# Three pairs of chunks by seven block products in the last stage, their later weight sums by accumulating DMAs

## The chip, the cores and the metric

The kernel runs on one core of a Trainium2 chip. The metric is the device time of one execution in microseconds, of the slowest core (there is one). Five engines with their own in-order queues work side by side: TensorE (PE) multiplies, VectorE (DVE), ScalarE (ACT) and GpSimd (POOL) do elementwise work, SyncE (SP) issues most DMAs. They wait for each other by semaphores only.

## The reference, cut to what matters

Two transformer blocks in float32 on x of 1 x 256 x 1024. The last stage, which the change is about, is the squared-ReLU MLP that ends the second block:

```python
h2 = rmsnorm_2(x, norm_mlp_g[l])                                             # 256 x 1024
up = jnp.square(jax.nn.relu(jnp.einsum('bsd,df->bsf', h2, w_up[l])))         # w_up 1024 x 4096
x = x + jnp.einsum('bsf,fd->bsd', up, w_down[l])                             # w_down 4096 x 1024
```

The two gated stages, which the change touches at their ends only, are `h + 0.5 * swiglu(rmsnorm(h), w_gu, w_down)` with 2816 hidden columns.

## The kernel before

**Split products.** Every float32 weight tile of 128 x 4 x 512 (1 MB, a *unit*) is used as hi + lo: ScalarE copies it to a rounded type (`split_hi`, L1101 to L1114), VectorE subtracts (`split_lo`, L1816 to L1822). A product of a block is then three matmuls for each of four 128-row slices (`portion`, L2628 to L2658): hi x hi, lo weight, lo data. So a unit used for one token half is 12 matmuls of 512 columns, for both halves 24. hi and lo lie in a ring of three slots for all units in order: `split_hi(n)` waits until TensorE is through with unit n - 3 (`used`, n - 2).

**The last stage.** The 4096 hidden columns are eight chunks of 512. A chunk costs two *up* units (two halves of the 1024 input rows) and two *down* units. A chunk's result is squared by ScalarE, written as 16-bit planes (`planes_from`, L1346), turned by a DMA transpose on SyncE (`flip_last`, L721), merged by VectorE (`last_merge`, L2093) and split again (`last_hi`, L1378, `last_lo`, L2103) before its down units. `last_order` (L106) fixes TensorE's order by hand; down units of two chunks earlier stand between the up work.

**Pairs.** `PAIRS` names the chunks i for which i and i + 1 are computed together: the 2 x 2 blocks of tokens and columns, with the input rows in two halves, by seven products of blocks instead of eight (`product`, L2854). Products p1, p2 and p3 take a loaded block of w_up; p5, p6, p7 and p4 take sums of blocks, T1 to T4, made by VectorE in place in six buffers `last_operand` (`weight_sum`, L1869 to L1889: buffer 4 = 2 + 0, 5 = 3 + 4, 2 = 3 + 2, 1 = 1 + 5). Partial results pass through PSUM bank G[0] and `xn`: ScalarE's `keep` (L1178) copies the bank after p1, p6 and p7; p6, p7 and p4 then add on to the same bank, and TensorE waits for the copy before each; VectorE's `add_product` (L1916) adds p2, p5 and p3; `square` (L1365) squares the four finished blocks. Before, chunks 2 and 3 and chunks 6 and 7 are such pairs; 0, 1, 4 and 5 are plain. In this text u(i,b) and d(i,b) are up and down units.

**What sets the order.** `pair_chunks` and `plain_chunks` write out ScalarE's order (L1388, L1424) and VectorE's (L2118, L2153) by hand; SyncE's order of loads and transposes is a list (L950 to L993). In a pair that is not the first, ScalarE has before: d(i-2,0), keep 0, p6, d(i-2,1), square 0, p7, last_hi(i-1), keep 1, p5, p4, keep 2; VectorE: d(i-2,0), add 0, p6, d(i-2,1), merge(i-1), p7, T4, last_lo(i-1), p5, p4. GpSimd has no work in this stage. The first three sums of the second pair are made in the plain chunks before it.

**The gated stages' ends.** SyncE loads the last down units, then the first unit of w_in for the next stage, and then issues the two transposes of chunk 9 (L864 to L869, L922 to L927), whose merge is L1939, whose lo is L1947 and whose matmuls are L2806.

Of the kernel before, what the change touches and what calls it, by code (L numbers as in the profile page):

```python
# [42 lines left out]
W = 512  # L43
# [34 lines left out]
PAIRS = (2, 6)  # L78
# [49 lines left out]
LAST_PAIR = len(PAIR_AT) - len(PAIRS)  # L128

# [176 lines left out]
class Pairs:  # L306


    def __init__(self, sem):
        self.b_in = [sem(f"pairs_b_in{j}") for j in range(4)]  # L310
        self.t_made = sem("pairs_t_made")
        self.s_made = sem("pairs_s_made")
        self.s_hi = sem("pairs_s_hi")
        self.s_lo = sem("pairs_s_lo")
        self.kept = sem("pairs_kept")
        self.added = sem("pairs_added")


def program(nc, a, out):
    ctx = ExitStack()  # L320
    with ctx:
# [327 lines left out]
        def _(sp_eng):  # L649
# [34 lines left out]
            def block_free(j, b):  # L684
# [3 lines left out]
                elif PAIR_AT[j][1] == PAIRS[1] or j in (1, 3):  # L688
# [49 lines left out]
            def gated_weights(w_gu, w_down, f, beside=lambda k: None):  # L738
# [62 lines left out]
                dn(10)  # L801

# [61 lines left out]
            for c, (first, width, _) in enumerate(IN1):  # L864
                for half in range(2):
                    columns(a["w_in"], U_M1 + 2 * c + half, first, half, width)
                    if (c, half) == (0, 0):
                        flip(ffns[0], 9, 1)
                        flip(ffns[0], 9, 0)  # L869
# [50 lines left out]
            for c, (first, _) in enumerate(IN2):  # L920
                for half in range(2):
# [3 lines left out]
                    if (c, half) == (0, 0):  # L925
                        flip(ffns[1], 9, 1)
                        flip(ffns[1], 9, 0)  # L927
# [33 lines left out]
            last_block(LAST_PAIR + 1, 0)  # L961
            last_load("d", 1, 1)
            last_load("u", 4, 0)
            flip_last(2, 0)
            last_block(LAST_PAIR + 1, 2)
            last_block(LAST_PAIR + 1, 1)
            last_load("u", 4, 1)
            flip_last(2, 1)
            last_block(LAST_PAIR + 1, 3)
            last_load("d", 2, 0)  # L970
            flip_last(3, 1)
            flip_last(3, 0)
            last_load("d", 2, 1)
            last_load("u", 5, 0)
            last_load("u", 5, 1)
            flip_last(4, 0)
            flip_last(4, 1)
            last_load("d", 3, 0)
            last_load("d", 3, 1)
            last_load("d", 4, 0)  # L980
            flip_last(5, 0)
            last_load("d", 4, 1)
            flip_last(5, 1)
            last_load("d", 5, 0)
            last_load("d", 5, 1)
            last_load("d", 6, 0)
            flip_last(6, 0)
            last_load("d", 6, 1)
            flip_last(6, 1)
            last_load("d", 7, 0)  # L990
            flip_last(7, 1)
            flip_last(7, 0)
            last_load("d", 7, 1)  # L993
# [93 lines left out]


        @block.scalar
        def _(act):  # L1090
# [10 lines left out]
            def split_hi(n, width=W):  # L1101
# [5 lines left out]
                elif KINDS[n] in OPERAND:  # L1107
                    act.wait_ge(pairs.t_made, 4 * pair_of(n) + {"p5": 1, "p6": 2, "p7": 3, "p4": 4}[KINDS[n]])
# [279 lines left out]
            def pair_chunks(j):  # L1388

                i = PAIR_AT[j][1]  # L1390
                split_hi(unit_of("d", i - 2, 0))
                if j == LAST_PAIR:
                    plain_planes(1, 0)
# [26 lines left out]
                last_hi(i)  # L1420
                square(j, 3)
                split_hi(unit_of("d", i - 1, 1) + 2)

            def plain_chunks(i):  # L1424

                split_hi(unit_of("d", i - 2, 0))
                last_hi(i - 1)
                split_hi(unit_of("d", i - 2, 1))
                plain_planes(i, 0)
                split_hi(unit_of("u", i + 1, 0))  # L1430
                plain_planes(i, 1)
                split_hi(unit_of("u", i + 1, 1))
                split_hi(unit_of("d", i - 1, 0))
                last_hi(i)
                split_hi(unit_of("d", i - 1, 1))
                plain_planes(i + 1, 0)
                split_hi(unit_of("d", i - 1, 1) + 1)
                plain_planes(i + 1, 1)
                split_hi(unit_of("d", i - 1, 1) + 2)

            def last_ffn():
# [9 lines left out]
                for i in range(2, NF2, 2):  # L1451
                    if i in PAIRS:
                        pair_chunks(PAIR_AT.index((2, i)))
                    else:
                        plain_chunks(i)
# [351 lines left out]
        def _(dve):  # L1807
# [61 lines left out]
            def weight_sum(j, t):  # L1869
# [10 lines left out]
                elif t == 2:  # L1880
                    dve.wait_ge(pairs.b_in[3], UNIT_IN * (j + 1))
                elif t == 4:
                    dve.wait_ge(pairs.b_in[1], UNIT_IN * (j + 1))
                    dve.wait_ge(lo_done, pair_unit(j, "p2") + 1)
                if t > 1:
                    dve.wait_ge(pairs.t_made, 4 * j + t - 1)
# [231 lines left out]
            def pair_chunks(j):  # L2118

                i = PAIR_AT[j][1]  # L2120
                split_lo(unit_of("d", i - 2, 0))
                if j == LAST_PAIR:
                    for m in (3, 2, 4):
                        sum_lo(2, m)
# [3 lines left out]
                    weight_sum(j, 4)  # L2128
                    split_lo(unit_of("p7", i))
                    last_merge(i - 1)  # L2130
                else:
# [5 lines left out]
                    weight_sum(j, 4)  # L2137
                    last_lo(i - 1)
                split_lo(unit_of("p5", i))
                if j == LAST_PAIR:  # L2140
# [9 lines left out]
                last_lo(i)  # L2150
                split_lo(unit_of("d", i - 1, 1) + 2)

            def plain_chunks(i):  # L2153

                j = LAST_PAIR + len([x for x in PAIRS if x < i])
                split_lo(unit_of("d", i - 2, 0))
                last_merge(i - 1)
                weight_sum(j, 1)
                split_lo(unit_of("d", i - 2, 1))
                last_lo(i - 1)  # L2160
                split_lo(unit_of("u", i + 1, 0))
                weight_sum(j, 2)
                split_lo(unit_of("u", i + 1, 1))
                last_merge(i)
                split_lo(unit_of("d", i - 1, 0))
                weight_sum(j, 3)
                last_lo(i)
                split_lo(unit_of("d", i - 1, 1))
                split_lo(unit_of("d", i - 1, 1) + 1)
                split_lo(unit_of("d", i - 1, 1) + 2)  # L2170

            def last_ffn():
# [8 lines left out]
                for i in range(2, NF2, 2):  # L2181
                    if i in PAIRS:
                        pair_chunks(PAIR_AT.index((2, i)))
                    else:
                        plain_chunks(i)
# [438 lines left out]
        def _(pe):  # L2624
# [208 lines left out]
            def plain_up(i):  # L2833

                for u in range(2):
                    n = unit_of("u", i, u)
                    use(n)
                    for t in range(NT):
                        if i > 1 and u == 0 and i % 2 == 0:

                            if t == 0:
                                pe.wait_ge(last.acted, acted_before(i))
                            else:
                                pe.wait_ge(pairs.added, 3 * (LAST_PAIR + len([x for x in PAIRS if x < i])) - 2)
                        elif i > 1 and u == 0 and t == 0:

# [417 lines left out]
```

## Time and profile before

| | us |
|---|---|
| median of 3 runs | 980.93 (980.13 to 981.02) |
| the profiled execution, its own time | 980.98 |
| its span in the trace | 979.2 |
| TensorE busy | 971.3 |
| VectorE busy | 764.8 |
| ScalarE busy | 658.5 |
| GpSimd busy | 117.4 |

Times in the trace count from the span's start. A timeline row gives the start, the duration, the engine, the line and the operation with its tiles, and in brackets how long the engine was idle before it and what released it. Matmuls overlap in the pipeline, so a row's duration (0.39 us) is longer than the distance between two starts. Instructions on ScalarE and VectorE overlap too by about 0.1 us.

### The profile page before, as it was taken

How to read it: one execution, taken by the hardware profiler on the slowest of the kernel's cores; microseconds unless marked ns; L12 is line 12 of the kernel's file. 1: busy time of each engine (PE TensorE's matmuls, PEld its weight loads, DVE VectorE, ACT ScalarE, POOL GpSimd, SP SyncE). 2: the span in 40 equal slices, each digit the busy share in tenths (PEclk: the TensorE clock that was granted, in tenths of full speed). 3: DMA queues.
4: the chain of work that ended last, by engine and by line, in shares of the span. 5: the costliest groups of instructions: out<-in, count | busy, mean ns of one | idle time of the engine just before them, and what ended most of it. 6: DMA issues, size and time to landing. Idle time of an engine off the chain costs nothing.

```text
span 979.2 us, 12257 instructions
## 1 busy us (share of the span) xinstructions
PE 971.3 (99%) x4528; PEld 796.9 (81%) x4528; DVE 764.8 (78%) x1010; ACT 658.5 (67%) x887; POOL 117.4 (12%) x109
## 2 busy tenths in 40 slices
PE   8999999999999999999999999999999999999998
PEld 7788888888777788888888788888888888888887
DVE  5898797768987666888797677787689878977675
ACT  7766575677666536766566586868875548877782
POOL 0000000022300000000000041169903001000000
PEclk9999999999999999999999999999999999999999
DMA  8998948696444546986926587667666654695532
GB/s 262 314 294 281 281 122 240 199 320 196 133 151 148 172 129 215 260 268 213 267 67 213 180 243 230 164 181 208 201 214 215 239 191 151 210 321 172 189 111 94
DMA packets 167589, 202.12 MB, mean 206 GB/s; under 512 B 58081, under 2 KB 113770, under 8 KB 167402
## 3 DMA queue, kind: packets, MB, share of 16 engines
q1 hardware_dynamic: 166938, 201.21, 65.9%
q8 instruction: 36, 0.59, 0.2%
q14 instruction: 23, 0.19, 0.1%
q10 hardware_dynamic: 592, 0.14, 0.1%
HBM read 182.45 MB, written 5.77 MB: 192 GB/s over the span
## 4 chain that ended last, share of the span: by engine, by line
PE 91%; DVE 2%; DMA 2%; issue 1%; ACT 1%; SPq 1%; POOL 0%; ACTq 0%; DVEq 0%
PE bank L2653 22%; PE bank L2655 22%; PE bank L2654 22%; PE bank L2806 4%; PE bank L2808 4%; PE bank L2807 4%; PE bank L2924 3%; PE bank L2925 3%; PE bank L2926 3%; DMA halves_t<-halves 2%; PE bank L2668 1%; PE bank L2960 1%; PE bank L3075 1%; DMA raw<-in_ffn_w_gu 1%; DVE lo L1838 0%
## 5 line engine op out<-in xcount | busy, mean ns | idle before, releaser
L2653 PE MATMUL bank<-hi,xh 128*128 128x512 f32 (+1 forms) x824 | 328.2, 398 | 1.0 <-DVE lo L2254 0.9
L2655 PE MATMUL bank<-hi,xl 128*128 128x512 f32 (+1 forms) x824 | 320.7, 389 | 0.0
L2654 PE MATMUL bank<-lo,xh 128*128 128x512 f32 (+1 forms) x824 | 320.1, 388 | 0.0
L1821 DVE TENSOR_TENSOR lo<-raw,hi 128x2048 fp32r<-128x2048 f32 (+1 forms) x87 | 198.5, 2287 | 60.8 <-ACT hi L1114 60.5
L1114 ACT ACTIVATE hi<-raw 128x2048 fp32r<-128x2048 f32 (+1 forms) x90 | 170.6, 1902 | 83.7 <-PE bank L2655 36.7
L2653 PEld LDWEIGHTS bank<-hi,xh 128*128 128x128 f32 x824 | 154.9, 188 | 34.4 <-issue 2.7
L2655 PEld LDWEIGHTS bank<-hi,xl 128*128 128x128 f32 x824 | 154.8, 188 | 32.7
L2654 PEld LDWEIGHTS bank<-lo,xh 128*128 128x128 f32 x824 | 155.1, 188 | 29.7
L1838 DVE TENSOR_TENSOR lo<-raw,hi 128x1024 fp32r<-128x1024 f32 (+1 forms) x108 | 132.2, 1234 | 43.4 <-ACT hi L1123 42.9
L1123 ACT ACTIVATE hi<-raw 128x1024 fp32r<-128x1024 f32 x102 | 104.5, 1051 | 10.1 <-PE bank L2655 10.1
L2806 PE MATMUL bank<-hi,hh 128*128 128x512 f32 x176 | 69.2, 393 | 1.2 <-DVE hl L1947 1.2
L2808 PE MATMUL bank<-hi,hl 128*128 128x512 f32 x176 | 68.6, 390 | 0.0
L2807 PE MATMUL bank<-lo,hh 128*128 128x512 f32 x176 | 68.5, 389 | 0.0
L1821 DVE TENSOR_TENSOR lo<-first_operand,hi 128x2048 fp32r<-128x2048 f32 x28 | 64.1, 2288 | 3.6 <-ACT hi L1114 3.5
L1114 ACT ACTIVATE hi<-first_operand 128x2048 fp32r<-128x2048 f32 x28 | 53.6, 1916 | 17.0 <-PE bank L2655 11.8
L1025 POOL TENSOR_TENSOR small<-small 128x1 f32<-128x1 f32 x10 | 8.5, 851 | 366.4 <-DVE small L1845 346.4
L2925 PE MATMUL bank<-lo,last_hh 128*128 128x512 f32 (+1 forms) x130 | 50.1, 386 | 0.0
L2926 PE MATMUL bank<-hi,last_hl 128*128 128x512 f32 (+1 forms) x130 | 50.1, 386 | 0.0
L2924 PE MATMUL bank<-hi,last_hh 128*128 128x512 f32 (+1 forms) x130 | 50.1, 386 | 0.0
L1032 POOL TENSOR_TENSOR rstd_q<-ss_q,small 128x8 f32<-128x8 f32 x16 | 34.6, 2166 | 88.5 <-DVE ss_q L2331 88.3
L2806 PEld LDWEIGHTS bank<-hi,hh 128*128 128x128 f32 x176 | 33.1, 188 | 8.5 <-issue 2.0
L1821 DVE TENSOR_TENSOR lo<-last_operand,hi 128x2048 fp32r<-128x2048 f32 x14 | 32.0, 2288 | 8.8 <-ACT hi L1114 8.8
(315 smaller groups left out, 1498.3 us busy)
## 6 DMA issues: line engine op xcount, KB each, us to landing
raw<-in_w_in SPq DMA_DIRECT2D x48, 1024.0 KB
raw<-in_ffn_w_gu SPq DMA_DIRECT2D x50, 512.0 KB
raw<-in_ffn_w_down SPq DMA_DIRECT2D x22, 1024.0 KB
first_operand<-in_ffn_w_gu SPq DMA_DIRECT2D x32, 512.0 KB
raw<-in_w_down SPq DMA_DIRECT2D x16, 1024.0 KB
raw<-in_w_out SPq DMA_DIRECT2D x8, 1024.0 KB
last_operand<-in_w_up SPq DMA_DIRECT2D x8, 1024.0 KB
raw<-in_w_up SPq DMA_DIRECT2D x8, 1024.0 KB
```

What stands on the lines that cost most here:

```text
L1114: nc.scalar.activation(hi[s][:, :, 0:width], whole(n)[:, :, 0:width], ACT.Copy).then_inc(hi_done, 1)
L1123: ins = nc.scalar.activation(hi[s][:, cut, :], raw[r % RING][:, cut, :], ACT.Copy)
L1821: nc.vector.tensor_tensor(lo[s][:, :, 0:width], whole(n)[:, :, 0:width], hi[s][:, :, 0:width].bitcast(F32), ALU.subtract).then_inc(lo_done, 1)
L1838: ins = nc.vector.tensor_tensor(lo[s][:, cut, 0:width], raw[slot(n) % RING][:, cut, 0:width], hi[s][:, cut, 0:width].bitcast(F32), ALU.sub ...
L2653: nc.tensor.matmul(o, sh, wh, start=first and j == 0, stop=False, skip_group_check=onto)
L2654: nc.tensor.matmul(o, sh, wl, start=False, stop=False, skip_group_check=onto)
L2655: ins = nc.tensor.matmul(o, sl, wh, start=False, stop=last and j == 3, skip_group_check=onto)
L2806: nc.tensor.matmul(dst, sh, wh, start=i == 0 and k == 0, stop=False)
L2807: nc.tensor.matmul(dst, sh, wl, start=False, stop=False)
L2808: ins = nc.tensor.matmul(dst, sl, wh, start=False, stop=end)
L2924: nc.tensor.matmul(dst, sh, wh, start=begin, stop=False)
L2925: nc.tensor.matmul(dst, sh, wl, start=False, stop=False)
```

## The change

`PAIRS` gets chunk 4, so chunks 2 to 7 are three pairs in a row and only 0 and 1 are plain; `plain_chunks` goes. For every pair of the last stage T4 is made by an accumulating DMA from buffer 5 into buffer 1, for the second and third pair T3 by an accumulating DMA that adds the block of w_up in HBM to buffer 2; both are issued by GpSimd, in order. T1 and T2 stay on VectorE. VectorE's order in a later pair is T2, p6, d(i-2,1), add 0, p7, merge(i-1), p5, last_lo(i-1), p4, d(i-1,0), add 1, T1 of the next pair, p3. At a pair's end the hi copies of the next p1, p2 and of d(i,0) come ahead of the last square. The transposes of gated chunk 9 are issued ahead of the first w_in load.

```diff
-PAIRS = (2, 6)
+PAIRS = (2, 4, 6)
+SUMS_MADE = [4 * min(j, LAST_PAIR) + (0 if j <= LAST_PAIR else 3 + 2 * (j - LAST_PAIR - 1))
+             for j in range(len(PAIR_AT) + 1)]
@@ gated_weights, SyncE (taken out of the two loops over w_in behind it)
                 dn(9)
                 dn(10)
+                flip(f, 9, 1)
+                flip(f, 9, 0)
@@ last stage, SyncE
+            for j in range(LAST_PAIR, len(PAIR_AT)):
+                i = PAIR_AT[j][1]
+                if i < NF2 - 2:
+                    last_block(j + 1, 0)
+                last_load("d", i - 1, 1)
+                last_load("d", i, 0)
+                flip_last(i, 0)
+                if i < NF2 - 2:
+                    last_block(j + 1, 2)
+                    last_block(j + 1, 1)
+                last_load("d", i, 1)
+                flip_last(i, 1)
+                if i < NF2 - 2:
+                    last_block(j + 1, 3)
+                last_load("d", i + 1, 0)
+                flip_last(i + 1, 1)
+                flip_last(i + 1, 0)
+            last_load("d", NF2 - 1, 1)
@@ GpSimd, behind norm_rstd(4)
+            def third_sum(j):
+                pool.wait_ge(pairs.t_made, SUMS_MADE[j] + 1)
+                i = PAIR_AT[j][1] + 1
+                nc.gpsimd.dma_start(last_operand[2][:, :, :], col_view(a["w_up_2"])[:, 4:8, i * W:i * W + W],
+                                    accum_op=ALU.add).then_inc(pairs.t3_in, UNIT_IN)
+            def fourth_sum(j):
+                pool.wait_ge(pairs.t_made, SUMS_MADE[j] + 2)
+                pool.wait_ge(lo_done, pair_unit(j, "p2") + 1)
+                nc.gpsimd.dma_start(last_operand[1][:, :, :], last_operand[5][:, :, :],
+                                    accum_op=ALU.add).then_inc(pairs.t4_in, UNIT_IN)
+            fourth_sum(LAST_PAIR)
+            third_sum(LAST_PAIR + 1)
+            fourth_sum(LAST_PAIR + 1)
+            third_sum(LAST_PAIR + 2)
+            fourth_sum(LAST_PAIR + 2)
@@ ScalarE, end of pair_chunks
-                last_hi(i)
-                square(j, 3)
-                split_hi(unit_of("d", i - 1, 1) + 2)
+                if j + 1 < len(PAIR_AT):
+                    split_hi(unit_of("d", i - 1, 1) + 2)
+                    last_hi(i)
+                    split_hi(unit_of("d", i, 0))
+                    square(j, 3)
+                else:
+                    last_hi(i)
+                    square(j, 3)
+                    split_hi(unit_of("d", i - 1, 1) + 2)
@@ VectorE, pair_chunks, a pair that is not the first
-                    add_product(j, 0)
+                    weight_sum(j, 2)
                     split_lo(unit_of("p6", i))
                     split_lo(unit_of("d", i - 2, 1))
+                    add_product(j, 0)
+                    split_lo(unit_of("p7", i))
                     last_merge(i - 1)
-                    split_lo(unit_of("p7", i))
-                    weight_sum(j, 4)
+                    split_lo(unit_of("p5", i))
                     last_lo(i - 1)
                 split_lo(unit_of("p4", i))
                 split_lo(unit_of("d", i - 1, 0))
                 add_product(j, 1)
+                if more:
+                    weight_sum(j + 1, 1)
                 split_lo(unit_of("p3", i))
...
+                if more:
+                    split_lo(unit_of("d", i - 1, 1) + 2)
+                    last_lo(i)
+                    split_lo(unit_of("d", i, 0))
```

## Rows read from the trace of the kernel before

**Rows 1.** The page's parts 1 and 4: busy time, and the chain by engine.

```profile
PE 971.3 (99%) x4528; PEld 796.9 (81%) x4528; DVE 764.8 (78%) x1010; ACT 658.5 (67%) x887; POOL 117.4 (12%) x109
PE 91%; DVE 2%; DMA 2%; issue 1%; ACT 1%; SPq 1%; POOL 0%; ACTq 0%; DVEq 0%
```

**Rows 2.** Windows: stretch, length, busy us of each engine, clock, DMA share, GB/s.

```profile
818.46:870.14 51.68, 51.68 (x229) 42.79 (x228) 43.67 (x31) 46.22 (x47) 0.00 (x0) 1.00 0.67 214
870.14:913.66 43.52, 43.52 (x193) 36.04 (x192) 31.83 (x18) 27.91 (x25) 0.00 (x0) 1.00 0.66 224
913.66:954.46 40.80, 40.80 (x181) 33.78 (x180) 31.60 (x20) 33.16 (x30) 0.00 (x0) 1.00 0.40 123
```

**Rows 3.** Timeline of TensorE: first matmuls of u(4,0) and of p1 of chunk 6.

```profile
870.14 0.39 PE L2653 MATMUL bank<-hi,xh 128*128 128x512 f32 x1
...
913.66 0.39 PE L2653 MATMUL bank<-hi,xh 128*128 128x512 f32 x1
```

**Rows 4.** Timeline of ScalarE in the pair of chunks 6 and 7.

```profile
913.92 1.92 ACT L1114 ACTIVATE hi<-raw 128x2048 fp32r<-128x2048 f32 x1 [3.50 <-PE bank L2926]
...
921.19 0.70 ACT L1374 ACTIVATE xn<-xn,small 128x512 f32<-128x512 f32 x1
...
922.59 1.06 ACT L1350 ACTIVATE last_halves<-xn 128x1024 uint16<-128x1024 uint16 x1
924.82 1.92 ACT L1114 ACTIVATE hi<-last_operand 128x2048 fp32r<-128x2048 f32 x1 [1.18 <-PE bank L2926]
926.64 1.14 ACT L1385 ACTIVATE last_hh<-last_hid_t 128x512 fp32r<-128x512 f32 x2
927.68 0.58 ACT L1186 ACTIVATE xn<-bank 128x512 f32<-128x512 f32 x1
```

**Rows 5.** Timeline of VectorE in the same pair.

```profile
919.37 0.69 DVE L1922 TENSOR_TENSOR xn<-bank,xn 128x512 f32<-128x512 f32 x1 [1.21 <-PE bank L2655]
919.98 2.28 DVE L1821 TENSOR_TENSOR lo<-last_operand,hi 128x2048 fp32r<-128x2048 f32 x1
922.18 2.29 DVE L1821 TENSOR_TENSOR lo<-raw,hi 128x2048 fp32r<-128x2048 f32 x1
924.38 1.35 DVE L2099 COPY last_hid_t<-last_halves_t 128x2048 uint16<-128x2048 uint16 x1
926.77 2.29 DVE L1821 TENSOR_TENSOR lo<-last_operand,hi 128x2048 fp32r<-128x2048 f32 x1 [1.04 <-ACT hi L1114]
928.98 2.29 DVE L1888 TENSOR_TENSOR last_operand<-last_operand 128x2048 f32<-128x2048 f32 x1
...
940.87 2.28 DVE L1821 TENSOR_TENSOR lo<-last_operand,hi 128x2048 fp32r<-128x2048 f32 x1
```

**Rows 6.** TensorE's waits; SyncE's timeline; the chain around 541 us; the first turned tile.

```profile
PE bank L2806 <- DVE hl L1947: 1.2, 2, 1.0
...
533.27 3.27 SPq L681 DMA_TRANSPOSE halves_t<-halves  x2
...
534.58 6.60 DMA halves_t<-halves
...
544.31 0.47 PE bank L2806
DMA to landing us min/median/max: 2.3/4.6/10.7
```

**Rows 7.** SyncE's and ScalarE's timeline near 890 us; landing times of last_halves_t.

```profile
888.25 3.51 SPq L719 DMA_DIRECT2D raw<-in_w_down  x3
894.34 1.92 ACT L1114 ACTIVATE hi<-raw 128x2048 fp32r<-128x2048 f32 x1 [5.44 <-DMA raw<-in_w_down]
DMA to landing us min/median/max: 2.7/2.9/6.5
```

**Rows 8.** Timeline of VectorE near 750 us, and of GpSimd beside it.

```profile
744.59 4.86 POOL L1084 TENSOR_TENSOR xc<-xc,grt 128x256 f32<-128x256 f32 x3 [33.36 <-DVE xc L2576]
746.17 2.68 DVE L1821 TENSOR_TENSOR lo<-raw,hi 128x2048 fp32r<-128x2048 f32 x1
```

More of the change, by code:

```diff
@@ L687, in block_free @@
                     sp_eng.wait_ge(*((k_pv, NH), (k_rl, 2), (k_ri, 8), (k_rl, 2))[b])
-                elif PAIR_AT[j][1] == PAIRS[1] or j in (1, 3):
+                elif j > LAST_PAIR:
+                    sp_eng.wait_ge(lo_done, pair_unit(j - 1, ("p1", "p4", "p7", "p3")[b]) + 1)
+                    if b == 0:
+                        sp_eng.wait_ge(pairs.t_made, SUMS_MADE[j - 1] + 1)
+                    elif b == 3:
+                        sp_eng.wait_ge(pairs.t_made, SUMS_MADE[j])
+                elif j in (1, 3):
                     sp_eng.wait_ge(lo_done, pair_unit(j - 1, ("p1", "p4", "p7", "p3")[b]) + 1)
@@ L1107, in split_hi @@
                 elif KINDS[n] in OPERAND:
-                    act.wait_ge(pairs.t_made, 4 * pair_of(n) + {"p5": 1, "p6": 2, "p7": 3, "p4": 4}[KINDS[n]])
+                    j = pair_of(n)
+                    if KINDS[n] == "p4" and j >= LAST_PAIR:
+                        act.wait_ge(pairs.t4_in, UNIT_IN * (j - LAST_PAIR + 1))
+                    elif KINDS[n] == "p7" and j > LAST_PAIR:
+                        act.wait_ge(pairs.t3_in, UNIT_IN * (j - LAST_PAIR))
+                    else:
+                        act.wait_ge(pairs.t_made, SUMS_MADE[j] + {"p5": 1, "p6": 2, "p7": 3, "p4": 4}[KINDS[n]])
                 else:
@@ L1450, in last_ffn @@
                 last_hi(0)
[L1451 to L1455, printed above, removed]
+                for j in range(LAST_PAIR, len(PAIR_AT)):
+                    pair_chunks(j)
                 split_hi(UNITS - 2)
@@ L1881, in weight_sum @@
                     dve.wait_ge(pairs.b_in[3], UNIT_IN * (j + 1))
+                    if j > LAST_PAIR:
+                        dve.wait_ge(pairs.t4_in, UNIT_IN * (j - LAST_PAIR))
                 elif t == 4:
@@ L1885, in weight_sum @@
                 if t > 1:
[L1886 removed]
+                    dve.wait_ge(pairs.t_made, SUMS_MADE[j] + t - 1)
                 dst, left, right = ((4, 2, 0), (5, 3, 4), (2, 3, 2), (1, 1, 5))[t - 1]
@@ L2120, in pair_chunks @@
                 i = PAIR_AT[j][1]
-                split_lo(unit_of("d", i - 2, 0))
+                more = j + 1 < len(PAIR_AT)
                 if j == LAST_PAIR:
+                    split_lo(unit_of("d", i - 2, 0))
                     for m in (3, 2, 4):
@@ L2149, in pair_chunks @@
                 split_lo(unit_of("d", i - 1, 1) + 1)
[L2150 to L2170, printed above, removed]
+                if more:
+                    split_lo(unit_of("d", i - 1, 1) + 2)
+                    last_lo(i)
+                    split_lo(unit_of("d", i, 0))
+                else:
+                    last_lo(i)
+                    split_lo(unit_of("d", i - 1, 1) + 2)
             def last_ffn():
@@ L2180, in last_ffn @@
                 sum_lo(2, 1)
[L2181 to L2185, printed above, removed]
+                for j in range(LAST_PAIR, len(PAIR_AT)):
+                    pair_chunks(j)
                 split_lo(UNITS - 2)
@@ L2838, in plain_up @@
                     for t in range(NT):
[L2839 to L2845, printed above, removed]
-                            pe.wait_ge(pairs.added, 3 * (LAST_PAIR + len([x for x in PAIRS if x < i])))
                         ins = portion(n, t, (G, X)[i % 2][t], xh, xl, 4 * u, u == 0, u == 1)
```

69 lines of the change are left out of this document (7 added, 62 removed).

## The prediction

> **What bounds the kernel now.** Three views, in this order. The page first: TensorE is busy for 971.3 of 979.2 us and the chain that ended last is TensorE for 91%, so any matmul that goes is worth its time, as long as nothing makes TensorE wait for more than that [rows 1]. Then the windows of the last stage: between 818.46 and 976 us TensorE has no gap at all, at full clock, but in the pair of chunks at the stage's end (913.66 to 954.46, 40.80 us) VectorE is busy for 31.60 and ScalarE for 33.16 us; in the pair at its start they have 43.67 and 46.22 of 51.68 us; in the plain chunks between, 31.83 and 27.91 of 43.52 us [rows 2]. Then the timelines of ScalarE and VectorE inside such a pair, since these two queues run strictly in the order written and each feeds the other: which instruction stands before which decides whether TensorE is fed [rows 4, 5]. The last pair of before is the nearest thing the trace has to a pair that follows a pair.
>
> **The matmuls: minus 2.72 us.** The pair window holds 180 matmuls of 512 columns (84 of products, 96 of four down units) in 40.80 us: 0.2267 us each [rows 2, 3]. The plain chunks 4 and 5 need 96 + 96, that is 43.52 us, and as seven products 84 + 96, 40.80 us. 43.52 - 40.80 = 2.72 us less on TensorE. A product is 12 x 0.2267 = 2.72 us, a down unit 5.44 us.
>
> **The transposes moved ahead of a load: minus 1.2 us.** In both gated stages SyncE issues the first w_in load before the two transposes of chunk 9. In the second stage the transposes are issued at 533.27, the second of them lands 6.60 us after its start at 534.58, behind about 3 MB of loads; VectorE's merge waits for it, then come hh and hl, and TensorE stands for 1.0 us until 544.31; in the first stage for 0.2 us. These are the 1.2 us of two waits in all [rows 6]. With the load behind them only two 1 MB loads are ahead; the stage's other transposes land in a median of 4.6 us, which makes the second land near 539.2, 2 us earlier, more than the 1.0 us of the stall. I take all 1.2 us. The load itself is now issued behind the transposes, at 533.27 + 3.27 = 536.5; the first of three loads in a row was there 6.1 us after its issue [rows 7], so it is there at 542.6. At 544.31 TensorE only begins the matmuls of chunk 9, and those of chunks 9 and 10, 5.4 us each, come before the unit is due: near 555, with 4.2 us for its hi and lo before it. It hides; without that cover it would cost the 3 to 5 us by which it moved. Bounds: 0 to 1.2 us of gain.
>
> **The sums of weights.** The first pair loses its fourth sum on VectorE (one 2.2 us step [rows 5]), and gets the first sum of the next pair ahead of p3's lo split. In the last pair of before that split begins at 940.87 and ends at 943.16, while p3 is due on TensorE at 913.66 + 32.64 = 946.30: 3.1 us to spare against 2.2 [rows 5], nothing on the path. Sums three and four of the later pairs go to GpSimd's queue as accumulating DMAs of 1 MB. The trace has none. GpSimd has nothing else queued behind them in this stage. Bounds: as fast as a plain 1 MB load, 6.1 us with two more behind it (issued from 888.25, hi copy at 894.34 [rows 7]), and three such passes for reading the source, reading the destination and writing, 18.3 us. By the plan below the shortest cover is 18.5 us for the fourth sum (876.83, when the second sum ends, to 895.34, hi of p4) and 27 us for the third. Both bounds are hidden; I take 8 to 12 us, nearest the first row.
>
> The Trainium skill (DMA: Bandwidth & Descriptors, SWDGE vs HWDGE vs iDMA) says that an accumulating DMA can only be made by GpSimd's software path, and its table of bandwidth has 6.15 us for 1 MB on that path; by that figure too the sums are covered, and the forecast stays.
>
> **The order in a pair that follows a pair.** This is the step that decides. Take S = 870.14, where p1 of chunks 4 and 5 starts on TensorE as u(4,0) does now [rows 3]. Without a stall p6 is due at S + 4 x 2.72 = 881.02, d(2,1) at 883.74, p7 at 889.18, p5 at 891.90, p4 at 894.62. Now the two queues, with the steps of before's last pair:
> - hi of d(2,0) needs the slot of d(1,1), free at S: it starts 0.26 us later (913.92 against 913.66 [rows 3, 4]), 870.40. Its lo starts 1.95 us after it (924.82 to 926.77 [rows 4, 5]): 872.35.
> - The new order puts the second sum behind that lo: lo steps take 2.20 us (919.98 to 922.18), so 874.55, ending 2.28 later at 876.83. p6's operand is this sum, so hi of p6 starts at 876.87, lo at 878.82, and ends at 881.11. TensorE is 0.2 us late. In before the sum was long made, and lo of p6 began at 919.98, S + 6.32 against S + 8.68 now.
> - VectorE now has lo of p6, lo of d(2,1) (881.02), and only then add_product (883.22, ends 883.90). In before it stood ahead of both (919.37, S + 5.71). ScalarE's order is unchanged: square 0 waits for it, and stands ahead of hi of p7. Its three steps take 2.46 us (921.19 to 923.65): 883.94 to 886.42. In before it ran at S + 7.53, now at S + 13.80.
> - hi of p7 886.45, lo 888.40 to 890.69. VectorE's merge of chunk 3 was ahead of p7's lo (924.38), now it is behind it: 890.60 to 891.95. ScalarE has last_hi(3) behind hi of p7, waiting for that merge, 891.98, and behind it keep 1, 1.04 us later (926.64 to 927.68): 893.02 to 893.6. TensorE may not start p7 before keep 1 has copied the bank that p7 adds to. So p7 starts at 893.7 instead of 889.18: 4.5 us late (0.2 of them from p6).
> - hi of p5 follows keep 1 by 0.5 us (its 0.58 less the overlap): 893.52, lo 895.47 to 897.76; TensorE 897.85, another 1.4 us. hi of p4 follows at once, 895.34, but VectorE has last_lo(3) (two steps, 1.20 us) between: lo of p4 898.87 to 901.16; TensorE 901.3 instead of 894.62, another 0.7 us.
> The pair is late by 6.7 us. Behind it d(3,0)'s lo ends at 903.4 and is due at 904.0, and nothing more waits. The slack ends there and the third pair begins at 870.14 + 40.80 + 6.7 = 917.6 with the same order, so it loses the same: 13.4 us for the two. The last pair of before didn't lose them since its first three sums, its early add_product and its early merge fit before p7. After a stall the first three matmuls took 0.1 us more (0.47 for the first one at 544.31 against 0.39 [rows 6]): eight restarts would be 0.8 us; part is hidden since the two other queues set the pace, so it goes into the range.
>
> **The sum.** The profiled execution took 980.98 us, 0.05 above the median of 980.93. 980.98 - 2.72 - 1.2 + 13.4 = 990.5; against the median 990.4 us, 1.0% slower. What can move it within the likeliest case: plus 1.2 us if the transposes land no earlier than now; minus 4 if the 6.7 us per pair are 2 too many; plus 0.8 for restarts; plus 0.4 us for each of a few VectorE instructions that run beside GpSimd's work (2.68 us for one lo split beside GpSimd at 746.17 [rows 8], against 2.29 at 922.18 [rows 5]), plus 2 for transposes that queue behind an accumulating DMA (landing 2.7 to 6.5 us now [rows 7], where the merges of chunks 2 and 4 have 2 to 3 us of room). 986 to 996 us.
>
> The Trainium skill (SBUF — State Buffer, Who interferes with whom) states that a VectorE instruction with both inputs in SBUF contends only with a GpSimd instruction that reads SBUF, and that a copy in its two-port mode keeps GpSimd from writing descriptors. By the first half the 0.4 us would not come back here; by the second a merge of 1.34 us could hold an accumulating DMA up by as much, far less than the cover's 18.5 us less the 8 to 12 that I take. The sum is the same by either.
>
> **Rivals.**
> - *The engines have room, so the order costs nothing.* One pair asks VectorE for 11 lo splits of 2.20, two sums of 2.20, two merges and two last_lo of about 1.2 and three adds of 0.6 us [rows 5], some 35 us, and ScalarE for 11 hi copies of 1.82, four squares of 2.5, two last_hi of 1.04 and three keeps of 0.5 us [rows 4], some 34 us, in 40.80; now nothing waits at 31.60 and 33.16 [rows 2]. If the merge and add_product waits are absorbed, only the savings are left: 980.98 - 2.72 - 1.2 = 977.1, faster. It decides if keep 1 ends by 889.1, 4.5 us before my plan. Against it: every link above is a wait in the code and a duration from a row, and the first start of the chain (870.40) is set by TensorE itself.
> - *The accumulating DMA outlasts its cover.* Against the 18.5 us nothing in the trace sets a firm price. From there each further microsecond holds hi of p4 back in all three pairs; p4's lo has 1.6 us to spare behind it (897.3 to 898.87), so TensorE pays from 20 us on: at 25 us about 5 us each, 990.4 + 15 = 1005 us. For it: loads already fill the DMA engines at 0.66 of the middle window [rows 2], and the sum reads and writes SBUF.
> - *Part of the chain.* Only p7's wait comes, the two behind it are taken up, or the transposes' gain is larger: 2 x 4.5 instead of 2 x 6.7, 986; with one more link out, 982.
>
> **How the numbers follow.** A run of this kernel can't tell less than 0.2% (2 us) from no change. Chances: the forecast 0.75 (986 to 996), DMA outlasts 0.12, part of the chain 0.06 (982 to 986), room on the engines 0.07. Range 985 to 997: it leaves out most of the DMA case and the faster case, about 2 in 10. Faster 0.07, same 0.01, slower 0.92.
>
> **What would show it.** TensorE's idle rows in 870 to 990: none before p1 of the second pair, about 4.3 us before p7 with keep (L1186's line) as the releaser, 1.4 before p5, 0.6 before p4, twice each. ScalarE's square waiting for VectorE's add_product for 3.4 us, and last_hi for the merge for 3.7 us. The wait of L2806 on hl gone. ScalarE's wait for the accumulated operands zero. It is wrong if p7 starts at its due time, if hi of p4 is released by GpSimd's DMA, or if transposes land over 7 us after their issue.

## The result and the profile after

The changed kernel takes 992.0 us (median of four runs, 991.45 to 998.11) beside 980.53 us of the kernel before (979.94 to 981.02): a ratio of 1.0131, 95% interval 1.0091 to 1.0172. The forecast was 990.4 us, range 985 to 997. One of the four runs, 998.11 us, is 6 us longer than the other three; no trace of it exists, so its cause is open. The profiled execution took 992.29 us, with a span of 990.5 us; the page has for it, against [rows 1]:

```profile
PE 974.1 (98%) x4516; PEld 797.0 (80%) x4516; DVE 773.3 (78%) x1015; ACT 666.3 (67%) x893; POOL 124.5 (13%) x114
PE 88%; DVE 5%; ACT 3%; issue 1%; DMA 1%; POOL 0%; SPq 0%; ACTq 0%; DVEq 0%
```

Twelve matmuls are gone, yet TensorE is busy for 2.8 us more (some matmuls run at the lower clock, see below), and its unbusy time has grown from 7.9 us (979.2 - 971.3) to 16.4 (990.5 - 974.1). The windows say where, against [rows 2]. The second and third begin at the pairs' first p1, the third ends where the pair's last down unit starts, and the first begins 0.51 us ahead of its p1 (816.31) (columns: stretch, length, busy us of TensorE, its weight loads, VectorE, ScalarE, GpSimd, then clock, DMA share, GB/s):

```profile
815.80:867.99 52.19, 52.19 (x232) 43.20 (x232) 44.94 (x31) 45.24 (x44) 2.38 (x2) 1.00 0.79 223
867.99:917.18 49.19, 44.24 (x181) 35.39 (x179) 34.24 (x23) 33.35 (x30) 2.19 (x2) 0.93 0.89 250
917.18:960.32 43.14, 38.15 (x157) 30.23 (x157) 30.61 (x19) 30.56 (x28) 0.88 (x1) 0.96 0.51 134
```

The first pair is whole: 52.19 - 0.51 = 51.68 us, as before. The second, planned at 40.80 us, takes 49.19; it and the third have TensorE idle for 4.95 and 4.99 us, and a granted clock below 1, though VectorE and ScalarE are busy for less than 36 us of either window: they wait in turns, which no busy share shows. TensorE's timeline has all its gaps behind 862 us (in brackets: idle time, and what ended it):

```profile
891.59 0.77 PE L2643 MATMUL bank<-hi,last_sum_h 128*128 128x512 f32 x1 [4.12 <-ACT xn L1203]
917.18 0.50 PE L2643 MATMUL bank<-hi,xh 128*128 128x512 f32 x1 [0.84 <-DVE lo L1824]
929.27 0.50 PE L2643 MATMUL bank<-hi,last_sum_h 128*128 128x512 f32 x1 [0.74 <-DVE lo L1824]
941.84 0.77 PE L2643 MATMUL bank<-hi,last_sum_h 128*128 128x512 f32 x1 [4.07 <-ACT xn L1203]
949.28 0.50 PE L2643 MATMUL bank<-hi,xh 128*128 128x512 f32 x1 [0.17 <-DVE lo L1824]
```

These are p7 of both later pairs (behind `keep`, now L1203), p1 and p6 of the third pair, and its p4. The forecast had no wait before p1. Behind p7's wait in the second pair the windows view shows a granted clock of 0.50:

```profile
891.59:896.85 5.26, 5.26 (x13) 4.10 (x14) 3.57 (x4) 3.45 (x2) 0.00 (x0) 0.50 0.69 222
```

ScalarE's timeline in the second pair, to be laid beside [rows 4]:

```profile
874.73 1.92 ACT L1131 ACTIVATE hi<-last_operand 128x2048 fp32r<-128x2048 f32 x1 [1.56 <-DVE last_operand L1893]
...
881.81 0.73 ACT L1391 ACTIVATE xn<-xn,small 128x512 f32<-128x512 f32 x1 [3.35 <-DVE xn L1927]
...
884.32 1.92 ACT L1131 ACTIVATE hi<-last_operand 128x2048 fp32r<-128x2048 f32 x1
889.81 1.15 ACT L1402 ACTIVATE last_hh<-last_hid_t 128x512 fp32r<-128x512 f32 x2 [3.58 <-DVE last_hid_t L2104]
890.87 0.58 ACT L1203 ACTIVATE xn<-bank 128x512 f32<-128x512 f32 x1
```

VectorE's, beside [rows 5]:

```profile
872.41 2.29 DVE L1893 TENSOR_TENSOR last_operand<-last_operand 128x2048 f32<-128x2048 f32 x1
876.68 2.29 DVE L1824 TENSOR_TENSOR lo<-last_operand,hi 128x2048 fp32r<-128x2048 f32 x1 [1.99 <-ACT hi L1131]
878.88 2.29 DVE L1824 TENSOR_TENSOR lo<-raw,hi 128x2048 fp32r<-128x2048 f32 x1
881.09 0.68 DVE L1927 TENSOR_TENSOR xn<-bank,xn 128x512 f32<-128x512 f32 x1
886.27 2.29 DVE L1824 TENSOR_TENSOR lo<-last_operand,hi 128x2048 fp32r<-128x2048 f32 x1 [4.50 <-ACT hi L1131]
888.48 1.30 DVE L2104 COPY last_hid_t<-last_halves_t 128x2048 uint16<-128x2048 uint16 x1
```

Read them as one relay: `weight_sum` (L1893) lets ScalarE's hi of p6 go at 874.73; VectorE waits 1.99 us for that hi, makes two lo splits and only then `add_product` (881.09), for which ScalarE has stood 3.35 us; VectorE waits 4.50 us for hi of p7, ScalarE 3.58 us for the merge behind it, and `keep` comes at 890.87, with TensorE idle since 887.09. All pair starts lie 2.15 us earlier than planned (p1 at 867.99 instead of 870.14); shifted by that, the forecast had hi of p7 at 884.30, keep at 890.87, p7 at 891.55; the trace has 884.32, 890.87, 891.59.

The second stage's transposes on SyncE, now ahead of the loads; beside the row at 533.27 of [rows 6]. TensorE's wait for hl (L2806 before, L2796 now) is in none of its wait rows any more:

```profile
532.36 2.53 SPq L685 DMA_TRANSPOSE halves_t<-halves  x2
534.95 9.45 SPq L663 DMA_DIRECT2D raw<-in_w_in  x3
```

### The profile page after: what moved, and what is told of

It is laid out like the page before. It is cut to its first block, busy times and chain, and to the rows that moved or that the text cites. A ratio compares the mean times of both kernels' runs of the same rounds, so it can differ in the third digit from the quotient of the medians.

```text
span 990.5 us, 12265 instructions
## 1 busy us (share of the span) xinstructions
PE 974.1 (98%) x4516; PEld 797.0 (80%) x4516; DVE 773.3 (78%) x1015; ACT 666.3 (67%) x893; POOL 124.5 (13%) x114
## 4 chain that ended last, share of the span: by engine, by line
PE 88%; DVE 5%; ACT 3%; issue 1%; DMA 1%; POOL 0%; SPq 0%; ACTq 0%; DVEq 0%
PE bank L2643 22%; PE bank L2645 21%; PE bank L2644 21%; PE bank L2798 4%; PE bank L2796 4%; PE bank L2797 4%; DVE lo L1824 2%; PE bank L2906 2%; PE bank L2905 2%; PE bank L2907 2%; ACT hi L1131 1%; PE bank L2658 1%; PE bank L2939 1%; PE bank L3054 1%; DMA last_halves_t<-last_halves 1%
## 5 line engine op out<-in xcount | busy, mean ns | idle before, releaser
L2643 PE MATMUL bank<-hi,xh 128*128 128x512 f32 (+1 forms) x804 | 320.5, 399 | 1.8 <-DVE lo L1824 1.0
L2645 PE MATMUL bank<-hi,xl 128*128 128x512 f32 (+1 forms) x804 | 312.8, 389 | 0.0
L2644 PE MATMUL bank<-lo,xh 128*128 128x512 f32 (+1 forms) x804 | 312.1, 388 | 0.0
L1824 DVE TENSOR_TENSOR lo<-raw,hi 128x2048 fp32r<-128x2048 f32 (+1 forms) x83 | 189.4, 2286 | 49.5 <-ACT hi L1131 49.4
L1131 ACT ACTIVATE hi<-raw 128x2048 fp32r<-128x2048 f32 (+1 forms) x86 | 163.2, 1902 | 77.1 <-PE bank L2645 36.1
L2643 PEld LDWEIGHTS bank<-hi,xh 128*128 128x128 f32 x804 | 151.0, 188 | 35.6 <-issue 3.0
L2645 PEld LDWEIGHTS bank<-hi,xl 128*128 128x128 f32 x804 | 150.9, 188 | 32.0
L2644 PEld LDWEIGHTS bank<-lo,xh 128*128 128x128 f32 x804 | 151.2, 188 | 28.9
L2796 PE MATMUL bank<-hi,hh 128*128 128x512 f32 x176 | 69.0, 392 | 0.0
L1824 DVE TENSOR_TENSOR lo<-last_operand,hi 128x2048 fp32r<-128x2048 f32 x21 | 47.9, 2290 | 26.5 <-ACT hi L1131 26.5
L1131 ACT ACTIVATE hi<-last_operand 128x2048 fp32r<-128x2048 f32 x21 | 39.8, 1912 | 6.5 <-DVE last_operand L1893 4.1
```

What stands on the lines that cost most here:

```text
L1131: nc.scalar.activation(hi[s][:, :, 0:width], whole(n)[:, :, 0:width], ACT.Copy).then_inc(hi_done, 1)
L1824: nc.vector.tensor_tensor(lo[s][:, :, 0:width], whole(n)[:, :, 0:width], hi[s][:, :, 0:width].bitcast(F32), ALU.subtract).then_inc(lo_done, 1)
L2643: nc.tensor.matmul(o, sh, wh, start=first and j == 0, stop=False, skip_group_check=onto)
L2644: nc.tensor.matmul(o, sh, wl, start=False, stop=False, skip_group_check=onto)
L2645: ins = nc.tensor.matmul(o, sl, wh, start=False, stop=last and j == 3, skip_group_check=onto)
L2796: nc.tensor.matmul(dst, sh, wh, start=i == 0 and k == 0, stop=False)
```

## The experiments

All edits are to the changed kernel unless said. "Late" means against TensorE's own pace from the pair's first p1 (in the second pair p7 is due 19.04 us and d(3,0) 27.20 us behind it, the next p1 40.80; in the third pair the last down unit 35.36). For the changed kernel the lateness is 7.39 us at d(3,0), 1.0 more at p1 of the third pair, 7.78 more in the third pair: 16.17 in all.

**Only the merge, only the add, both ahead.** VectorE's order in later pairs:

```diff
                     weight_sum(j, 2)
+                    add_product(j, 0)
                     split_lo(unit_of("p6", i))
                     split_lo(unit_of("d", i - 2, 1))
-                    add_product(j, 0)
+                    last_merge(i - 1)
                     split_lo(unit_of("p7", i))
-                    last_merge(i - 1)
                     split_lo(unit_of("p5", i))
```

This is m3. m1 moves `last_merge` alone, m2 `add_product` alone.

> The changed kernel with one move in a later pair: VectorE merges chunk i-1 ahead of p7's lo split (as before the change), add_product stays late. Theory (order of the queues): keep 1 is free about 3.7 us earlier, p7 then waits for its lo alone, 1.6 us late instead of 4.6; idle before p7 about 1.5 us instead of 4.1, waits before p5 and p4 under 0.5: each pair 5 to 5.5 us shorter, 981 us. Rival (the engines are full, order is nothing): 992. Rival (the accumulating DMAs hold it): 992.

> The changed kernel with the other move alone: VectorE's add_product 0 directly behind the second sum, ahead of p6's lo, the merge stays behind p7's lo. Theory: square 0 starts 3.5 us earlier, hi of p7 starts when its slot is free, keep 1 ends near 2.4 us after p7's due time instead of 4.6; p5 and p4 late by 1.3 and 0.7 as forecast: each pair about 3 us shorter, 986 us. Rivals: 992.

> Both moves: second sum, add_product 0, p6, d(i-2,1), merge, p7, p5. Theory: p7, p5 and p4 on time; left are 0.2 us before p6 of the second pair, 1.0 before p1 and 1.2 before p6 of the third: 978 us, below the kernel before (980.5). Rival (engines full): TensorE's waits only move to other units, over 985. Rival (DMA): 992.

Measured: 990.18 us (ratio 1.0101, 1.0087 to 1.0115), 988.72 us (1.0086, 1.0064 to 1.0107; runs from 985.91 to 992.01) and 977.14 us (0.9969, 0.9958 to 0.998). m3 came near what was expected (978) and is faster than both kernels. Its two later pairs, from the windows view, have no idle TensorE and full clock; they take 0.6 us more than the 40.80 and 35.36 us that are due, where 2.4 us of waits were expected:

```profile
868.09:909.18 41.09, 41.09 (x182) 33.72 (x180) 35.76 (x23) 33.72 (x30) 2.19 (x2) 1.00 1.03 291
909.18:944.85 35.67, 35.67 (x157) 29.20 (x156) 29.70 (x19) 30.11 (x27) 0.88 (x1) 1.00 0.68 175
```

So with this order nothing of the loss is left, and the engines do have room for three pairs; m12 below separates the order from the DMA. The other two missed by 9 and 3 us, and not where the order acts: in the second pair of m1 p7 waits for 1.12 us instead of 4.12 and d(3,0) is 3.05 us late instead of 7.39, a gain of 4.3 us where 5 to 5.5 were planned; m2 has 0.67 and 3.29, a gain of 4.1 where 3 were planned. TensorE's timeline of m1 goes on, though:

```profile
888.38 0.50 PE L2643 MATMUL bank<-hi,last_sum_h 128*128 128x512 f32 x1 [1.12 <-DVE lo L1824]
...
918.17 0.79 PE L2643 MATMUL bank<-hi,xh 128*128 128x512 f32 x1 [6.42 <-DVE lo L1824]
```

The second gap is new. In the timeline of m1's other queues it goes back to a transpose:

```profile
900.35 1.30 POOL L1083 DMA_DIRECT2D last_operand<-in_w_up  x1 [24.71 <-DVE last_operand L1893]
...
900.67 1.24 SPq L736 DMA_TRANSPOSE last_halves_t<-last_halves  x1
...
912.83 1.32 DVE L2104 COPY last_hid_t<-last_halves_t 128x2048 uint16<-128x2048 uint16 x1 [7.91 <-DMA last_halves_t<-last_halves]
```

The transpose, issued 0.3 us behind the accumulating DMA of the third sum, takes 12.0 us to land (median 4.4), the third sum 18.2 us (10.2 in the pair before), and between 905 and 911 the DMA engines move 61 GB/s at a busy share of 1.42, and VectorE and ScalarE do nothing:

```profile
905.00:911.00 6.00, 6.00 (x28) 4.96 (x27) 0.00 (x0) 0.00 (x0) 0.00 (x0) 1.00 1.42 61
```

m2 has the same in its profiled execution of 990.14 us: 6.61 us before that p1, a transpose of 12.2 us, a third sum of 18.6 us. Two other runs of m2, 985.91 and 987.30 us, are near the expected 986; they have no trace, so that they escaped it is likely but not shown. This points to a second mechanism: an accumulating DMA and a transpose in flight together hold each other up. m10 below tests it.

**The transposes alone.** The kernel before, with only the change in the gated stages (the same two lines behind the first w_in load are taken out, in both stages):

```diff
                 dn(9)
                 dn(10)
+                flip(f, 9, 1)
+                flip(f, 9, 0)
```

> The kernel before with one edit of the change, the two transposes of gated chunk 9 ahead of the first load of w_in. Theory: both waits of L2806 for hl go (0.2 and 1.0 us in the trace), with the slow restart behind each 1.5 us in all: 979.0 us. Rival (the w_in load comes late and gives it back): 980.5 or more, with a ScalarE wait for raw<-in_w_in near 543 us.

Measured: 978.82 us against 980.18, ratio 0.9984 (0.9975 to 0.9993), that is 1.4 us faster by the medians; TensorE's wait for hl is gone. That is near the forecast's 1.2 us.

**The third sum issued later.** To keep it off the transposes, GpSimd first waits for one of them:

```diff
             def third_sum(j):
                 pool.wait_ge(pairs.t_made, SUMS_MADE[j] + 1)
+                pool.wait_ge(last.flip[1], 16 * (PAIR_AT[j - 1][1] + 1))
```

In the changed kernel (m5), on top of m1 (m8) and on top of m3 (m7):

> The changed kernel, but GpSimd issues the third sum only when the transpose of the second half of chunk 2 (4) has landed, so the accumulating DMA from HBM is no longer beside that transpose. Theory (the accumulating DMA slows the transpose beside it: in the changed kernel it landed 6.5 us after its issue and cost 1.0 us before p1 and 1.0 before p6 of the third pair; the waits before p7 are the queues' order): 990 us, the 4.1 us idle before p7 unchanged twice. Rival (the transpose is late by the plain loads ahead of it): 992, its landing stays over 6 us.

> The merge ahead of p7's lo, and the third sum issued late. The merge alone gave 990.2 us where 981 was expected: its pairs were 5 us shorter, but the transpose beside the third sum landed after 12 us and stopped TensorE for 6.4 us before p1 of the third pair. Theory (contention of the accumulating DMA with the transpose): that wait goes, 983.5 us. Rival (the wait comes from the new order, not from the DMA): 990.

> Both moves on VectorE and the third sum late. Theory: in the version with both moves (977.1) the transpose landed in 4.5 us and only 0.2 to 0.8 us of TensorE were lost before p1 and p6 of the third pair: 976.5 us. Rival (later landing of the third sum, 10 us after about 902, collides with the next two transposes and holds the merge of chunk 5): over 978.

Measured: 999.14 us (ratio 1.0231, 1.0184 to 1.0278), 994.12 us (1.0162, 1.0121 to 1.0204; its profiled execution was the longest of the four, 1004.19) and 1008.25 us (1.0293, 1.0253 to 1.0334). Three misses of 9 to 32 us. The edit moved the sum onto the next transposes rather than off them. m7 has the order of m3, in which TensorE doesn't wait, and differs from it by GpSimd's wait alone, so its loss comes from the sum's new place; rows of its ScalarE timeline, and then of its DMA view between 918 and 945 us (queue: packets, MB, share of 16 engines):

```profile
929.29 0.63 ACT L1393 ACTIVATE xn<-xn 128x512 f32<-128x512 f32 x1
951.02 1.06 ACT L1368 ACTIVATE last_halves<-xn 128x1024 uint16<-128x1024 uint16 x1 [21.10 <-DMA last_halves_t<-last_halves]
```

```profile
DMA packets 2536, 2.01 MB, mean 74 GB/s; under 512 B 1955, under 2 KB 1955, under 8 KB 2493
q1 hardware_dynamic: 1971, 0.63, 74.9%
q0 software_dynamic: 565, 1.38, 59.8%
```

In 27 us SyncE's queue (q1) moved 0.63 MB and GpSimd's (q0) 1.38 MB, and the packets' time adds up to more than all 16 engines have. The longest transpose landed after 28.2 us; the third sums after 21.7 and 24.4 (the view below), the fourth sums behind them after 22.3 and 29.1, and for the first of these ScalarE waited 1.95 us:

```profile
DMA to landing us min/median/max: 21.7/23.1/24.4
```

**The accumulation taken out.** m7 once more, with the third sum as a plain copy of the same block by the same queue at the same place; the addition is left out.

```diff
                 nc.gpsimd.dma_start(last_operand[2][:, :, :], col_view(a["w_up_2"])[:, 4:8, i * W:i * W + W],
-                                    accum_op=ALU.add).then_inc(pairs.t3_in, UNIT_IN)
+                                    ).then_inc(pairs.t3_in, UNIT_IN)
```

> As the version with both moves and the third sum late (1008 us), but GpSimd's DMA from HBM copies instead of adding: the block is not added to buffer 2, which leaves the addition of the third sum out in the two later pairs. Issue times, size and queue are the same. In the accumulating version this DMA took 22 to 24 us, and the transposes beside it up to 28, and TensorE waited 7.0 and 18.7 us. Theory (it is the accumulation, reading and writing the destination, that gets into the transposes' way): landing near 6 us, transposes back under 8, 977 us. Rival (any DMA of GpSimd's queue beside a transpose does it): landing over 15 us, 1000 us or more.

Measured: 976.75 us, ratio 0.9966 (0.9954 to 0.9978), against 1008.25 for m7. The first of the two is issued at 861.16 (861.41 in m7), so the traffic it meets is alike (the second, at 901.40 against 912.06, meets other traffic, since m7 is late by then); they land after 10 us instead of 21.7 and 24.4, and the transposes after at most 9.6 us:

```profile
DMA to landing us min/median/max: 10.0/10.1/10.2
```

It is the accumulating of this block that the transposes suffer from, neither GpSimd's queue nor the size nor the place. Whether the addition does it or the additional reading of buffer 2 isn't told apart. The fourth sums, from SBUF, still accumulate in m10; they took 7.7 to 9.6 us and held nothing up. My duration for the plain copy, 6 us, was wrong.

**TensorE kept busy in the gap before p7.** To price the lower clock:

```diff
                 n = unit_of(kind, i)
+                if kind == "p7" and j > LAST_PAIR:
+                    for _ in range(30):
+                        nc.tensor.transpose(X[1][:, 0:P], ident[:, :], ident[:, :])
                 use(n)
```

> The changed kernel, with 30 transposes of a 128 x 128 identity into an unused bank on TensorE ahead of its wait for p7 in the two later pairs, 3 to 3.5 us of work in the 4.1 us gap; nothing else differs. It tells what the clock costs: after the gap 13 matmuls started 0.43 us apart instead of 0.227, 2.6 us per pair. Theory A (most of it hides behind the waits for p5's and p4's lo, which were there in the forecast): 991, 0.7 us gained in the second pair, little in the third. Theory B (the clock is a cost of its own): 992 - 5 = 987. In both the granted clock stays 1.0 if the idle time is what lowers it.

Measured: 997.67 us, ratio 1.018 (1.0167 to 1.0194), a miss as a whole, but the second pair answers the question. TensorE's timeline of this kernel:

```profile
887.08 3.44 PE L2841 MATMUL bank<-ident 128*128 128x128 f32 x30
891.37 0.47 PE L2643 MATMUL bank<-hi,last_sum_h 128*128 128x512 f32 x1 [0.86 <-ACT xn L1203]
...
895.41 0.50 PE L2643 MATMUL bank<-hi,last_sum_h 128*128 128x512 f32 x1 [1.04 <-DVE lo L1824]
898.82 0.50 PE L2643 MATMUL bank<-hi,xh 128*128 128x512 f32 x1 [0.37 <-DVE lo L1824]
...
922.96 0.79 PE L2643 MATMUL bank<-hi,xh 128*128 128x512 f32 x1 [7.49 <-DVE lo L1824]
```

p7 starts 23.63 us behind p1 (23.60 in the changed kernel) and now runs at a granted clock of 1.00 (891.37 to 894.30), and the forecast's waits before p5 and p4, which the changed kernel doesn't show, appear: 1.04 and 0.37 us. d(3,0) comes 33.97 us behind p1 (901.71 - 867.74) instead of 34.59: the clock costs this pair 0.6 us net. The third pair starts behind the next wait and gives no such comparison. The last row is the DMA collision again (third sum 18.1 us, transpose 13.1).

**Sums on VectorE.** m9 is m3 with the third sum of the later pairs on VectorE, m11 all third and fourth sums (no accumulating DMA at all), m12 the changed kernel's order with the third sum in VectorE's idle time:

```diff
                     weight_sum(j, 2)
                     add_product(j, 0)
+                    weight_sum(j, 3)      # m9, m11: p7's operand, on VectorE
                     split_lo(unit_of("p6", i))
                     split_lo(unit_of("d", i - 2, 1))
                     last_merge(i - 1)
                     split_lo(unit_of("p7", i))
+                    weight_sum(j, 4)      # m11 alone
                     split_lo(unit_of("p5", i))
```

```diff
                     weight_sum(j, 2)
                     split_lo(unit_of("p6", i))
                     split_lo(unit_of("d", i - 2, 1))
                     add_product(j, 0)
+                    weight_sum(j, 3)      # m12
                     split_lo(unit_of("p7", i))
                     last_merge(i - 1)
```

> Both moves, and the third sum of the later pairs made by VectorE between add_product 0 and p6's lo instead of by a DMA from HBM; the fourth stays a DMA. Theory: the step of 2.2 us fills 1.4 us of idle time and makes p6 0.9 us late instead of 0.2 in each later pair (plus 1.4 us), and the transposes beside the DMA come faster (minus 0.5 to 1): 977.5 us, about as the version with both moves (977.1). Rival (VectorE is full): p7 and p5 late too, 980 or more.

> Both moves and no DMA sum at all: third sum between add_product 0 and p6's lo, fourth behind p7's lo and the merge in a later pair, and behind d(0,1)'s lo in the first, as before the change. Theory: p6 0.9 us late and p5 another 0.9 in each later pair: 3 us more than with both moves, 980 us; so the DMA sums are worth 2 to 3 us of VectorE's queue. Rival (VectorE has room for all of it): 977.

> The changed kernel's own order (add_product and merge late), but VectorE makes the third sum of the later pairs in the idle time between add_product 0 and p7's lo, 4.5 us long in the changed kernel, instead of the accumulating DMA from HBM. It tells apart how much of the 16.2 us of waits is order and how much is the DMA. Theory (order for the waits before p7, p5, p4; DMA for the 1.0 us before p1 and 1.0 before p6 of the third pair): TensorE waits 4.1 us before p7 twice as before, the two others under 0.3, 990 us. Rival (the DMA plays no part in the changed kernel): 992. Rival (the DMA is behind most of it): under 985.

Measured: m9 978.23 us (ratio 0.9976, 0.9966 to 0.9985), m11 978.99 us (0.9985, 0.9976 to 0.9994), m12 991.42 us (1.0113, 1.0096 to 1.013). m9 and m11 each show one wait of 0.72 us per later pair (m9 another of 0.24 us in the first): p6's lo, for which hi is already there, stands behind the third sum; m11's timeline has

```profile
921.11 0.50 PE L2634 MATMUL bank<-hi,last_sum_h 128*128 128x512 f32 x1 [0.72 <-DVE lo L1814]
```

m12 is what the order costs without a third sum by DMA. Its gaps on TensorE:

```profile
890.89 0.77 PE L2640 MATMUL bank<-hi,last_sum_h 128*128 128x512 f32 x1 [4.07 <-ACT xn L1199]
...
926.86 0.50 PE L2640 MATMUL bank<-hi,last_sum_h 128*128 128x512 f32 x1 [0.20 <-DVE lo L1820]
939.42 0.77 PE L2640 MATMUL bank<-hi,last_sum_h 128*128 128x512 f32 x1 [4.11 <-ACT xn L1199]
```

p7 keeps its wait of 4.1 us twice; the wait before p1 of the third pair (0.84 in the changed kernel) is gone and that before p6 down from 0.74 to 0.20. From p1 of the second pair to the last unit the two take 91.09 us (958.38 - 867.29) and 92.33 us (960.32 - 867.99): by these two executions 1.24 us of the 16.17 are the accumulating third sum, 14.9 the order with its clock (7.52 us late at d(3,0), 7.41 in the third pair). The transpose ahead of that p1 lands after 6.5 us in the changed kernel (issued at 905.25) and after 4.6 in m12 (904.69), and VectorE's merge waits for it 2.33 and 0.48 us.

## Why the prediction was right

Point by point, by its own steps:

- **Matmuls, -2.72.** Right: 4528 to 4516 matmuls at 0.2267 us.
- **Transposes ahead of the load, -1.2.** Right in cause and near in size: 1.4 us in m4. The changed kernel's p1 stands 2.15 us earlier than before; 0.48 of it is there at 158 us (a transpose issued at 157.99 instead of 158.47), where both kernels are still the same, and belongs to the execution, so that 1.67 us are left for the transposes; the load behind the transposes delayed nothing.
- **The order in a later pair, +6.7 twice.** The mechanism held in each link: square behind `add_product` (3.4 us forecast, 3.35 measured), last_hi behind the merge (3.7 and 3.58), `keep` and p7 (4.5 late forecast; 4.56 measured, 891.59 against 887.03). m3 is the test: the two instructions moved ahead, and nothing is lost. m1 and m2 show that each alone takes about 4 us out of the second pair. The rival with room on the engines was right on the room: with another order m3 has it.
- **Waits before p5 and p4, 1.4 and 0.6.** Wrong as rows: the second pair has none, the third 0.17 us. The half clock covers them: p7's twelve matmuls take 5.26 us (891.59 to 896.85) instead of 2.72, and by then p5's lo is made. In the third pair only the first seven start 0.42 us or more apart, and there the wait before p4 shows. m6 brings them back at 1.04 and 0.37. The pair's lateness comes out at 7.39 instead of 6.7, since the slow matmuls cost 0.6 us more than the waits that they cover. The forecast had 0.1 us per restart, from a stall of 1.0 us [rows 6].
- **Waits before p1 and p6 of the third pair.** Not forecast: 0.84 and 0.74 us, of which m12, without the accumulating third sum, keeps 0.20.
- **Accumulating DMAs, 8 to 12 us.** The third sums landed after 10.3 and 10.5 us, the fourth after 7.8 to 12.9; in the changed kernel ScalarE never waited for one. One sign of being wrong did come, a transpose that lands over 7 us after its issue:

```profile
DMA to landing us min/median/max: 2.7/3.9/9.9
```

It was a poor sign: the transposes of 9.9 us (of the issues from 862.80) and 7.8 (913.26) cost TensorE nothing, m3, where nothing waits, has 10.3, and it was one of 6.5 us that did. The forecast's small item, up to 2 us for transposes beside one, was real here (1.24), but sized by luck: it was bounded by waits in an ordinary queue, and the experiments show the same pair of transfers cost 6 to 19 us when they meet otherwise. The rival "the accumulating DMA outlasts its cover" had its seat elsewhere too: in m1, m2 and m5 to m8 it is the late transpose that stops TensorE, not p4's operand, though fourth sums of 19.0 to 29.1 us do occur in m5, m7 and m8, around and past the 20 us from which the forecast let TensorE pay.

The sum: 16.17 us of lateness measured against 13.4; the excess of 2.8 is 1.24 of the accumulating sum, 0.6 of the clock in the second pair (m6) and 0.9 that no run assigns; the clock can be part of it in the third pair, where its net cost wasn't measured. Against it stand the savings, 2.72 + 2.15 measured against 2.72 + 1.2 forecast. 979.2 - 4.87 + 16.17 = 990.5, the span, 1.8 us above the forecast's 979.2 - 2.72 - 1.2 + 13.4 = 988.7. That the total came so near is in part luck: 0.48 us of the savings belong to the execution and stand against waits that the forecast didn't have.

What stays open is when the two kinds of DMA slow each other. In m3 the third sum and a transpose are issued 0.07 us apart (898.18 and 898.25) and the transpose lands after 4.4 us; in m1 0.32 us apart, and it takes 12.0. In m3's 895 to 905 us plain loads are in flight as well; whether these or something else decides isn't settled, and a kernel that keeps the accumulating third sum carries that risk, m3 too, though its seven runs (976.76 to 978.34) show no sign of it. m9, which keeps only the fourth sum as an accumulating DMA, stands 0.7 us above m3 by the two ratios, whose intervals overlap, and never showed it in ten runs (977.37 to 978.71).

## What to carry to other kernels

Between two in-order queues that feed each other, write out who waits for whom with durations from rows: an instruction that another engine's head waits for (here an add of 0.6 us and a merge of 1.3) belongs ahead of long splits that have slack, and moving both ahead turned +1.3% into -0.3%. Busy shares can't tell: VectorE and ScalarE were less busy in the slow pair (34.24 and 33.35 of 49.19 us) than in the fast one (35.76 and 33.72 of 41.09). A transfer of a kind that the trace doesn't show is bounded by its company as well as by itself: try it beside the transfers it will meet before its shift between queues is relied on.

## What the hardware did that was not expected

- An accumulating DMA and a DMA transpose in flight together, in some meetings and not in others: accumulating 1 MB from HBM 10.4 us in the changed kernel, 17 to 26 us in m1, m2, m5, m6, m7 and m8 (one of the two or both); transposes 3.8 to 4.8 us in the median, the slowest of each of these runs 12 to 28 us, with the DMA engines in m7 counted as busy at 39 to 120 GB/s. Accumulating 1 MB from SBUF took 7.6 to 12.9 us, and 12.4 to 29.1 behind such a meeting (m5, m7, m8). A plain copy from HBM at the same place did none of it (10.1 us, transposes at most 9.6).
- GpSimd's plain 1 MB copy from HBM took 10.1 us beside SyncE's loads. The Trainium skill (DMA: Bandwidth & Descriptors, Bandwidth) has 6.15 us for 1 MB on that path, as busy time of the DMA engines without the making of descriptors; from issue to landing, under load, this case measures 1.6 times that, and the accumulating ones of the changed kernel took 0.3 us more.
- After 4.12 us without work TensorE's next thirteen matmuls started some 0.43 us apart instead of 0.227 (granted clock 0.50, its lower level of 1.2 GHz); after 4.07 us in the third pair it was only the next seven. After a gap of 1.12 us (m1) the clock stayed at 1.00 and the first alone was longer (0.50 in place of 0.39).
